# Moving the values' product of the prompt attention into the next sub-step, with a ring of four turned probabilities

## The reference, cut to what matters

```python
def _attend(q, k, v, mask, fq=None, fk_t=None):
    s = jnp.einsum('bqhd,bkhd->bhqk', q, k, preferred_element_type=F32)
    if fq is not None:
        s = s + (jnp.swapaxes(fq, 1, 2)[..., None] - fk_t[:, :, None, :])
    s = jnp.where(mask, s, -jnp.inf)
    p = jax.nn.softmax(s, axis=-1).astype(v.dtype)
    return jnp.einsum('bhqk,bkhd->bqhd', p, v)
```

## Time and profile before

| | us |
|---|---|
| median of 3 runs | 3636.93 |
| lowest and highest run | 3632.38, 3639.15 |
| the profiled execution | 3634.75 |
| its span, first to last instruction | 3633.1 |
| PE busy | 3259.5 (90%) |
| DVE, ACT, POOL busy | 1466.5, 896.6, 172.6 |
| mean granted PE clock | 0.961 |

### The profile page before, as it was taken

One profiled execution on the slowest core, in us unless ns is written; L12 is line 12 of the kernel. 1 busy time (PEld: TensorE's weight loads), 2 busy tenths in 40 slices (PEclk: granted clock), 3 DMA queues, 4 the chain that ended last, 5 costly groups with the idle time before them and its releaser, 6 DMA issues. The chain is left out here.

```text
span 3633.1 us, 52418 instructions
## 1 busy us (share of the span) xinstructions
PE 3259.5 (90%) x20718; PEld 2656.5 (73%) x20718; DVE 1466.5 (40%) x3367; ACT 896.6 (25%) x2006; POOL 172.6 (5%) x118
## 2 busy tenths in 40 slices
PE   0999986999999997988969999779999999977988
PEld 0788886777777775667858888767787777745867
DVE  5214234444444442354631143444434444423556
ACT  0221212333223332220121212223332233322110
POOL 0000000100110100000000000010111110000000
PEclk9999998999999998989979999889999999987999
DMA  5322216322333216764342222352223232096633
GB/s 197 110 87 94 84 54 201 86 69 59 88 93 88 83 39 173 228 234 151 127 157 89 91 96 68 115 158 68 69 72 91 85 94 66 30 262 205 217 136 110
DMA packets 405163, 419.73 MB, mean 116 GB/s; under 512 B 154561, under 2 KB 314177, under 8 KB 402561
## 3 DMA queue, kind: packets, MB, share of 16 engines
q1 hardware_dynamic: 371088, 376.87, 33.5%
q10 hardware_dynamic: 33840, 39.66, 3.3%
HBM read 291.17 MB, written 127.64 MB: 115 GB/s over the span
## 5 line engine op out<-in xcount | busy, mean ns | idle before, releaser
L351 PE MATMUL proj_acc<-proj_wh,keep_xh 128*128 128x512 f32 (+1 forms) x1296 | 501.7, 387 | 12.5 <-DVE proj_wl L326 12.5
L1066 PE MATMUL att_gacc<-att_gwh,keep_xh 128*128 128x256 f32 x1728 | 504.6, 292 | 2.5 <-POOL att_gwl L986 2.5
L352 PE MATMUL proj_acc<-proj_wl,keep_xh 128*128 128x512 f32 (+1 forms) x1296 | 500.4, 386 | 0.0
L353 PE MATMUL proj_acc<-proj_wh,keep_xl 128*128 128x512 f32 (+1 forms) x1296 | 500.2, 386 | 0.0
L1068 PE MATMUL att_gacc<-att_gwh,keep_xl 128*128 128x256 f32 x1728 | 486.8, 282 | 0.0
L1067 PE MATMUL att_gacc<-att_gwl,keep_xh 128*128 128x256 f32 x1728 | 485.9, 281 | 0.0
L1150 DVE COPY att_pt<-att_tr 128x256 f32<-128x256 f32 (+3 forms) x384 | 177.2, 461 | 620.9 <-PE att_tr L1031 620.6
L1093 ACT ACTIVATE att_p<-att_ss,att_stat 128x257 f32<-128x257 f32 (+9 forms) x384 | 249.4, 650 | 691.5 <-DVE att_stat L1143 691.5
L1020 PE MATMUL att_ss<-att_kt,att_qt 64*128 64x256 f32 (+9 forms) x1024 | 376.2, 469 | 1.3 <-DVE att_kt L1078 1.3
L1066 PEld LDWEIGHTS att_gacc<-att_gwh,keep_xh 128*128 128x128 f32 x1728 | 326.5, 189 | 17.2 <-issue 10.6
L1067 PEld LDWEIGHTS att_gacc<-att_gwl,keep_xh 128*128 128x128 f32 x1728 | 326.2, 189 | 0.0
(11 more groups left out here) (294 smaller groups left out, 4393.5 us busy)
## 6 DMA issues: line engine op xcount, KB each, us to landing
scratch_gates<-att_gout SPq DMA_DIRECT2D x216, 128.0 KB, 1.7
up_gates<-scratch_gates SPq DMA_DIRECT2D x18, 1536.0 KB, 8.0
proj_raw<-in_w_in SPq DMA_DIRECT2D x48, 512.0 KB, 3.7
att_graw<-in_w_in SPq DMA_DIRECT2D x48, 512.0 KB, 3.7
str_ka<-in_cache_a_kT SPq DMA_DIRECT2D x16, 1024.0 KB, 9.7
str_va<-in_cache_a_v SPq DMA_DIRECT2D x16, 1024.0 KB, 5.4
scratch_sg<-proj_out SPq DMA_DIRECT2D x54, 256.0 KB, 2.0
att_sg<-scratch_sg SPq DMA_DIRECT2D x24, 512.0 KB, 6.0
```

The costliest lines, as they stand in the source:

```text
L351: nc.tensor.matmul(bank, hi, wh[:, u, kt, 0:w], start=kt == 0, stop=False)
L352: nc.tensor.matmul(bank, hi, wl[:, u, kt, 0:w], start=False, stop=False)
L353: mm = nc.tensor.matmul(bank, lo, wh[:, u, kt, 0:w], start=False, stop=kt == KT - 1)
L1066: nc.tensor.matmul(gacc[:, 0:GW], hi, gwh[:, n % 2, k, :], start=k == 0, stop=False)
```

## The change

`value` of block a leaves the end of sub-step 2a + 1 and stands in sub-step 2a + 2, behind its turn and score and before the gate of block a. So PE's order is turn, score, value, gate, fill, prep in an even sub-step, and turn, score, fill, prep in an odd one. The last value of a unit falls in sub-step 0 of the next. The last of all stands behind the last turn. Since the turn of sub-step 2a + 2 is now copied before value a has read, `pt` has four slots (m % 4) where it had two.

```diff
             if before:
-                order += [("gate", *before), ("mix", *before)]
+                order += [("value", *before), ("gate", *before), ("mix", *before)]
             if m in fills:
                 order.append(("fill", n, fills.index(m)))
             if ahead and m >= 3 and m != 5:
                 order.append(("prep", n + 1, *ahead.pop(0)))
-            if m % 2:
-                order.append(("value", n, m // 2))
         assert not ahead
-    order += [("gate", len(UNITS) - 1, PT - 1), ("mix", len(UNITS) - 1, PT - 1)]
+    order += [("value", len(UNITS) - 1, PT - 1), ("gate", len(UNITS) - 1, PT - 1), ("mix", len(UNITS) - 1, PT - 1)]
     return order
...
-    p, pt = ph.sb("p", [P, 2, SEQ + 2]), ph.sb("pt", [P, 2, SEQ])
+    p, pt = ph.sb("p", [P, 2, SEQ + 2]), ph.sb("pt", [P, 4, SEQ])
...
-                                              pt[:, u, j * P:(j + 1) * P], start=j == 0, stop=j == len(tiles) - 1,
+                                              pt[:, (2 * a + u) % 4, j * P:(j + 1) * P], start=j == 0, stop=j == len(tiles) - 1,
...
-                    nc.scalar.activation(pt[:, m % 2, 0:512], tr[:, g % 2, :], ACT.Copy).then_inc(tr_taken[g % 2], 1)
+                    nc.scalar.activation(pt[:, m % 4, 0:512], tr[:, g % 2, :], ACT.Copy).then_inc(tr_taken[g % 2], 1)
...
-                nc.vector.tensor_copy(pt[:, m % 2, js[0] * P:(js[-1] + 1) * P], tr[:, g % 2, 0:len(js) * P])\
+                nc.vector.tensor_copy(pt[:, m % 4, js[0] * P:(js[-1] + 1) * P], tr[:, g % 2, 0:len(js) * P])\
```

## The result

The changed kernel takes 3681.56 us (median of 4 runs, 3670.98 to 3694.77) beside 3635.25 for the kernel before (4 runs, 3632.38 to 3639.15). The ratio is 1.0123, with a 95% interval of 1.0103 to 1.0142: 46 us slower. The forecast was slower, by 18 us, and its range ended at 3667.

A forecast was written before the change was run, and what follows sets the result against it. PE's own time was taken as the bound. Stops 45.2 us plus new seam waits 3 minus 30.4 removed gave +17.8 us: 3652.5 for the profiled execution, 3654.7 for the median, 0.5% slower, range 3641 to 3667.

The forecast's parts named there:

- What bounds the kernel: Attention stretches: PE's own time, busy 738 of 775 and 780 us at clock 0.99; only PE's waits can be won.
- Pipeline edges taken as 0: Into or out of a value: an edge costs 0.09 us more, two per value before and after, so 0.
- The seams: Between two units, sub-steps 14, 15, 0, 1: four PE waits go, 2.03 us a seam, 24.4 us for 12 seams.
- The scaling beside POOL's split: Gates' scaling, block 0 of kind a: contention costing at most 1 us by the rule, left out of the sum.
- The floor of kind b: Seams of kind b: chain through ACT, store, DMA and POOL, 8.2 us; removed in all 30.4 us, without it some 41.
- The stops: Turns 8, 10, 12, second groups waiting for the prep's copy: 0.88, 1.39 and 1.12 us added each, 45.2 us in all.
- the one that held up DVE's queue at mix: Rival at the seams: mix waits for a later gate, delaying exponentials; +11 us, 3666; chance 0.13.
- one of the forecast's signs of being wrong: In the changed kernel's profile: the forecast is wrong if PE waits for exponentials.
- The seams that win all of 41: Rival of no change: kind b's floor gives way, seams win 41 us, stops as computed, +7 us; chance 0.13.
- the stops that vanish: Faster rival, turns 8, 10, 12: second groups not stopped more than now, seams win as said; 3609 us, chance 0.08.
- The rival of no change: Seams of kind b: floor gives way; +7 us, or +3 with stops a tenth smaller; 3641 us, chance 0.13.
- all four: Rivals for the whole kernel: faster 3609 (0.08), no change 3641 (0.13), slower still 3666 (0.13), does nothing 3637 (0.03).

The follow-up runs named there:

- e1_seams: Only the values of blocks 0, 6 and 7 moved, against the kernel before: 3616.35 us, ratio 0.9950.
- e6_seams_load: Values of blocks 0, 6, 7 moved, next unit's second weights load issued behind the fifth fill instead of the last, against the kernel before: 3598.44 us, ratio 0.9887.
- e5_score_first: All values moved, PE doing the score ahead of the turn in sub-steps 8, 10 and 12, against the kernel before: 3618.55 us, ratio 0.9944.
- e3_value4: Only the value of block 4 moved, against the kernel before: 3669.33 us, ratio 1.0093.
- e9_value3: Only the value of block 3 moved, against the kernel before: 3646.24 us, ratio 1.0034.
- e2_stops: Only the values of blocks 3, 4 and 5 moved, against the kernel before: 3698.19 us, ratio 1.0173.
- e10_value4_filled: Only the value of block 4 moved, with 16 useless matmuls between turn 10's groups, against the kernel before: 3663.33 us, ratio 1.0081.

## Why the prediction was right or wrong, point by point

- **What bounds the kernel: right for PE's own time, and wrong in taking the clock of the earlier trace rows as fixed** (last point). The idle PE of the view of waits did understate the stops behind a prep, as the text said.
- **Pipeline edges taken as 0: right.** Values start 0.07 ahead of the end of the score, gates 0.07 ahead of the end of the value, turns 0.16 ahead of the end of the prep or fill. One reading in it is wrong: the value isn't alone on the halved array. In units of kind b a score, which uses 64 rows, also starts 0.07 ahead of the end of its turn (128 times in the trace of before), where it is 0.16 in kinds a and c. The count of the value's edges, and so the 0, doesn't change by that.
- **The seams: right.** 9.3 us from last fill to first where 9.2 was forecast. e1_seams won 23.5 us at full clock for the 27 of the sum. The scaling beside POOL's split, which the sum left out, cost 0.3 us in one seam of 12.
- **The floor of kind b: right.** In the changed kernel PE waits for POOL at eight first fills (13.3 us), all of them start 0.05 us behind POOL's end as forecast, and the early load took the wait away. The floor is worth more than the 10 us of the sum: e6_seams_load's attentions are 28.8 us shorter than e1_seams', of which 13.7 are the stretches of half clock at these seams.
- **The stops: right, each within 0.01 us.** The rule (copy's end, 0.06 to the load, 0.33 and 0.11 for each more) and the assumption that the copies end as far behind the prep as before both held. The waits for DVE's copy of a prep are 38 where 40 was written. e5_score_first shows it is the missing cover, not the value's place.
- **Rivals: the one that held up DVE's queue at mix did not come.** PE waits 0.8 us for exponentials in all, in two places; taken by the letter that is one of the forecast's signs of being wrong, but it is far from the 11 us of that rival. The seams that win all of 41 did not come either, nor the stops that vanish. (The rival of no change says 3641, while its own +7 gives 3644 on the median.) The measured 3681.56 lies above all four: none of them moved the clock.
- **The size of the sum: wrong, +18 for +46.** The step that failed is the clock: the sum priced each stop by PE's idle time alone, 45.2 + 3 - 30.4, and held the granted clock at the 0.99 of the earlier trace rows, a term put at nothing without a reason. That row was read as a condition of the stretch, not as something that the new stops could change. The runs showed 12 stretches at 0.50 in its place, a term of 25.6 us in the profiled execution. Of the miss in that execution, 51.3 - 17.8 = 33.5 us, 25.6 are this, 2.0 are stops less seams, and 5.9 lie outside the attention, within the spread of that part.

With the trace of before there was a hint. In the first layer the granted clock is 0.50 from 619.3 to 639.8 us, where PE waits 9.5 and 7.2 us at the start of the attention, and again from 1400.9, where the next phase starts with a wait of 9.0; it is 1.00 between. The Trainium skill says in "TensorE: Matmul & The Clock Gate" (What's actually happening) that the throttled clock is the default and that activity releases it. The traces here agree in direction: 1.2 GHz follows stops of PE of 1.3 to 2.3 us in many places, and with matmuls of no use in the same stop of turn 10 it stays at 2.4 GHz. With hindsight, the term to add can be estimated from the changed kernel's trace: a stretch of 3.4 us at half clock costs 1.7 us, at up to each of 14 turns 10 that is 0 to 24 us, and a range with it would have held the time. The trace of before alone gave no price.

What stays open: why some stops bring the clock down and others of the same length don't (8 of 14 turns 10 in the changed kernel, 10 of 14 in e3_value4, none at a turn 8 in e9_value3), and why it falls at seams of kind b with idle times of 0.6 us at most in e2_stops, e3_value4 and e10_value4_filled but not in the trace of the kernel before. Whether such stops make the time spread more is not shown: four runs of the changed kernel spread over 24 us, but four of e3_value4 over 6, and nine of the kernel before over 19.

## What to carry to other kernels

Before a step is taken out from between a producer and an engine that waits in order, ask what it was covering: here one step hid a PSUM bank's copy in three sub-steps of sixteen, and moving it cost more there than it won at the seams. Move it only where it wins, or put another step (a score, a fill) in its old place. And price a new stop of the matrix engine with the clock as well: filling it, even with work of no use, kept the clock up in the traces here, and won 4 to 10 us in the times.

## What the runs showed of the hardware that I had not expected

- A stop of turn 10, with PE idle for 1.74 us inside a busy stretch, was followed by 3.4 to 6.8 us at a granted clock of 0.50 in 8 of 14 places, even where PE is busy through all of that (window 686 to 689 above). With four stretches at seams it cost 25.6 us, more than the 19.8 of stops less gains.
- Where PE's idle times are only 0.3 to 0.6 us each (three within 7 us, at seams of kind b) the granted clock fell too, in e3_value4 at 1038.6, and did not at the same steps of the kernel before.
- 16 matmuls added to the stop of turn 10 in each of 14 places took the two attentions from 1582.7 to 1567.4 us (e3_value4 and e10_value4_filled).
